# Turning the experts' products on VectorE, with a new cut of gate and up over TensorE's column groups

## What is computed

```python
combine = sum over the top 2 of one_hot(top_idx) * softmax(top_vals)
for e in range(8):                      # w_gu[e]: 1024 x 5632, w_down[e]: 2816 x 1024, f32
    gu = xt @ w_gu[e]
    g, u = gu[..., :2816], gu[..., 2816:]
    y = y + combine[:, e:e + 1] * ((silu(g) * u) @ w_down[e])
```

## Time and profile before

| | |
|---|---|
| median of three runs | 1141.8 us (1140.04 to 1142.01) |
| span of the profiled execution | 1140.8 us; no time beside the span is recorded for it |
| TensorE busy | 1100.7 us, 96% |
| VectorE, ScalarE busy | 309.3 us (27%), 233.6 us (20%) |
| first and last gate-up matmul of the experts | 444.6 and 1085.5 us |
| moved by DMA | 343.6 MB, mean 301 GB/s |

### The profile page before, as it was taken

How to read it: one execution, slowest core, us unless ns; L and a number is a source line. 1 busy time by engine, 2 the same in 40 slices (tenths; PEclk the granted TensorE clock), 3 DMA queues, 4 the chain that set the end, 5 groups by cost and what they waited for, 6 DMA issues and landing times.

```text
span 1140.8 us, 21118 instructions
## 1 busy us (share of the span) xinstructions
PE 1100.7 (96%) x9437; PEld 606.5 (53%) x9438; DVE 309.3 (27%) x536; ACT 233.6 (20%) x361; POOL 9.5 (1%) x53
## 2 busy tenths in 40 slices
PE   7889999999999899999999999999999999999988
PEld 5556999998688445344343353343343343433436
DVE  4664544444642515001100110100210101001053
ACT  3363444443522612000000000000000000000033
POOL 3000000000000000000000000000000000000000
PEclk9979999999999999999999999999999999999999
DMA  9806555555312309999999999999999999999951
GB/s 335 304 1 208 199 184 186 187 184 182 111 75 74 148 1 372 415 389 316 415 420 419 417 420 419 417 419 397 417 419 419 417 419 419 417 420 419 417 213 39
DMA packets 114024, 343.61 MB, mean 301 GB/s; under 512 B 7757, under 2 KB 30858, under 8 KB 113930
## 3 DMA queue, kind: packets, MB, share of 16 engines
q1 hardware_dynamic: 113930, 342.22, 76.6%
HBM read 341.15 MB, written 1.05 MB: 300 GB/s over the span
## 4 chain that ended last, share of the span: by engine, by line
PE 92%; DVE 4%; DMA 2%; ACT 1%; issue 0%; SPq 0%; DVEq 0%; ACTq 0%
PE ps L1958 34%; PE ps L2009 13%; PE ps L1666 6%; PE ps L1668 6%; PE ps L1667 6%; PE ps L2014 4%; PE ps L1636 4%; PE ps L1815 2%; DMA wring<-in_w_exp_down 1%; PE ps L1982 1%; PE ps L1937 1%; PE ps L2027 1%; PE ps L1527 1%; PE ps L1797 1%; PE ps L1740 1%; PE ps L1549 1%
## 5 line engine op out<-in xcount | busy, mean ns | idle before, releaser
L1958 PE MATMUL ps<-wring,xg 128*32 128x512 f32 (+1 forms) x4704 | 417.1, 502 | 1.5 <-DVE e_h L1368 1.5
L1958 PEld LDWEIGHTS ps<-wring,xg 128*32 128x32 f32 x4704 | 156.4, 110 | 241.6 <-issue 197.6
L2009 PE MATMUL ps<-wring,ehT 128*32 128x512 f32 x1408 | 167.0, 593 | 1.6 <-DMA wring<-in_w_exp_down 1.0
L1666 PE MATMUL ps<-dn_high,w_high 128*128 128x256 f32 x352 | 99.7, 283 | 0.0
L1668 PE MATMUL ps<-dn_high,w_low 128*128 128x256 f32 x352 | 99.6, 283 | 0.0
L1667 PE MATMUL ps<-dn_low,w_high 128*128 128x256 f32 x352 | 99.6, 283 | 0.0
L1124 DVE TENSOR_TENSOR w_low<-ring,w_high 128x2048 fp32r<-128x2048 f32 x36 | 82.3, 2291 | 60.0 <-ACT w_high L695 60.0
L2009 PEld LDWEIGHTS ps<-wring,ehT 128*32 128x32 f32 x1408 | 45.7, 110 | 97.1 <-issue 92.2
L829 ACT COPY ehT<-ps 128x384 f32<-128x384 f32 (+1 forms) x24 | 10.5, 439 | 364.9 <-PE ps L1982 276.0
L1380 DVE COPY ehT<-ps 128x384 f32<-128x384 f32 (+3 forms) x24 | 10.8, 450 | 262.6 <-PE ps L1982 201.7
L695 ACT CAST w_high<-ring 128x2048 fp32r<-128x2048 f32 x36 | 68.1, 1901 | 30.3 <-PE ps L1668 30.3
(11 more groups left out here) (311 smaller groups left out, 990.1 us busy)
## 6 DMA issues: line engine op xcount, KB each, us to landing
wring<-in_w_exp_gu SPq DMA_DIRECT2D x128, 1024.0 KB, 17.6
wring<-in_w_exp_down SPq DMA_DIRECT2D x88, 1024.0 KB, 16.3
wring<-in_w_exp_gu SPq DMA_DIRECT2D x64, 768.0 KB, 14.3
ring<-in_w_ffn_gu SPq DMA_DIRECT2D x44, 512.0 KB, 5.0
ring<-in_w_ffn_down SPq DMA_DIRECT2D x11, 1024.0 KB, 4.8
ring<-in_w_ple_gate SPq DMA_DIRECT2D x4, 1024.0 KB, 4.8
ring<-in_w_q_b SPq DMA_DIRECT2D x4, 1024.0 KB, 4.8
ring<-in_w_o_b SPq DMA_DIRECT2D x4, 1024.0 KB, 4.9
```

What stands on the lines that cost most here:

```text
L1666: pe.matmul(out, high_l, high_r, start=first, stop=False)
L1958: return pe.matmul(ps[32 * quarter:32 * quarter + 32, bank, c0:c0 + 2 * nf * P], xg[:, member(n), k, 32 * b:32 * b + 32], w[:, :, f * P:(f ...
L2009: ins = pe.matmul(ps[32 * q:32 * q + 32, 3, :], turned(g, 2 * u + r, b, nb), w[:, r, half * 512:(half + 1) * 512], start=(g == 0 and u == ...
```

## The change

TensorE's turns are gone, and with them banks 5 and 6, `e_h`, the copies to `ehT` and the semaphores `e_T`, `e_T_low` and `e_T_high`. VectorE multiplies in place in `e_silu` and then transposes 32x32 blocks from `e_silu` to `ehT`, which has two halves, for even and odd groups. A block on partitions 32j to 32j+31 stays on these partitions, so the hidden columns that column group j holds must be those that the down weights have on partitions 32j to 32j+31: it takes, of each block of 128, the run of 32 columns number j. In all three groups each column group now has one matmul a tile, of 2 x 32 x (number of blocks) columns: 512 and 384. Silu and product are one instruction for each group. Silu waits until the transpose has left `e_silu`; the transpose waits until the down units that read its half of `ehT` are done.

```diff
+    def products_of(buf, g, nb):
+        n = 32 * GROUPS[g][1]
+        return buf[:, 0:nb * n].rearrange("p (b n) -> p b n", b=nb)
...
         def silu(g, n, kind, nb):
             used(kind, "gu", g, n - 1 if kind == "body" and g < 2 else n)
-            if g < 2:
-                act.activation(e_silu[:, 0:2 * nb].rearrange("p (b c) n -> p b (c n)", b=nb), ps[:, 0:nb, 0:256], ACT.Silu).then_inc(e_silu_done, 1)
...
+            if not (isinstance(n, int) and n * 3 + g == 0):
+                act.wait_ge(e_turned, n * 3 + g)
+            act.activation(products_of(e_silu, g, nb), gates_of(g, nb), ACT.Silu).then_inc(e_silu_done, 1)
...
         def product(g, n, nb):
             dve.wait_ge(e_silu_done, n * 3 + (g + 1))
...
+            h_ = products_of(e_silu, g, nb)
+            dve.tensor_tensor(h_, h_, ups_of(g, nb), ALU.mult).then_inc(e_act_done, 1)
+
+        def turned(g, n, nb, kind):
+            dve.wait_ge(e_act_done, n * 3 + (g + 1))
+            if g == 2:
+                dve.wait_ge(e_used, n * EUNITS + used_count(kind, "down", 0))
+            elif not (isinstance(n, int) and n == 0):
+                dve.wait_ge(e_used, n * EUNITS + (used_count(kind, "down", 2 - g) - EUNITS))
+            m = nb * 32 * GROUPS[g][1]
+            dve.transpose(ehT[:, g % 2, 0:m], e_silu[:, 0:m]).then_inc(e_turned, 1)
...
         def both_experts(n):                 # VectorE
-            turned_high(1, n, nb)
             product(2, n, nb)
+            turned(2, n, nb, "body")
...
-            turned_high(2, n, nb)
             product(0, n + 1, nb2)
+            turned(0, n + 1, nb2, "body")
             result_low(n, nb)
             add_expert(n, n)
-            turned_high(0, n + 1, nb2)
...
             product(1, n + 1, nb2)
+            turned(1, n + 1, nb2, "body")
...
         def gate_up(kind, g, n, nb, ks=range(KD)):          # TensorE
-                if g < 2:
-                    for b in range(nb):
-                        for j in range(4):
-                            ins = part(j, b, 2 * j, 2, b, 0, first)
...
+                nf = GROUPS[g][1]
+                columns = w.rearrange("p s (f j a) -> p j s f a", j=4, a=32)
+                for b in range(nb):
+                    for j in range(4):
+                        ins = pe.matmul(ps[32 * j:32 * j + 32, b, 0:64 * nf], xg[:, member(n), k, 32 * b:32 * b + 32], columns[:, j],
+                                        start=first, stop=last, skip_group_check=True)
...
         def last_groups(n, nb, kind):                       # TensorE
             down(kind, 0, n, nb)
-            gate_up(kind, 2, n, nb, range(0, 4))
-            turn(1, n, nb)
-            gate_up(kind, 2, n, nb, range(4, KD))
+            gate_up(kind, 2, n, nb)
             down(kind, 1, n, nb)
-            turn(2, n, nb)
             down(kind, 2, n, nb)
             scatter(n, nb)
```

More of the change, by code:

```diff
@@ L1439, in _ @@
         product(0, 0, TILES[0])
-        turned_high(0, 0, TILES[0])
+        turned(0, 0, TILES[0], "lead")
         turn_picks(1)
@@ L1443, in _ @@
         product(1, 0, TILES[0])
+        turned(1, 0, TILES[0], "lead")
         for n in range(E - 1):
@@ L1955, in gate_up @@
                 first, last = k == 0, k == KD - 1
[L1957 to L1961, removed]
-                    for b in range(nb):
-                        for j in range(4):
-                            ins = part(j, b, 2 * j, 2, b, 0, first)
-                else:
-                    for b in range(nb):
-                        for j in range(4):
-                            part(j, b, j, 1, b, 0, first)
-                    for b in range(nb):
-                        for j in range(2):
-                            ins = part((2 * b + j) % 4, b, 4 + j, 1, b // 2, 256, False)
@@ L1972, in gate_up @@
-                ins.then_inc(e_used, 1)
-        def turn(g, n, nb):
-            pe.wait_ge(e_act_done, n * 3 + (g + 1))
-            if not (g == 0 and isinstance(n, int) and n == 0):
-                pe.wait_ge(e_T_low, n * 3 + g)
-                pe.wait_ge(e_T_high, n * 3 + g)
-                if g == 0:
-                    pe.wait_ge(e_added, n * 2)
-            for i in range(2 * nb if g < 2 else nb + 1):
-                ins = pe.transpose(ps[:, 5 + i // nb, (i % nb) * P:(i % nb + 1) * P], e_h[:, i, :], ident[:])
-            if g == 2 and nb == 3:
-                ins = pe.transpose(ps[:, 6, P:P + 64], e_h[0:64, 4, :], ident[0:64, 0:64])
-            ins.then_inc(e_T, 1)
@@ L2008, in down @@
                             q = 2 * half + b
-                            ins = pe.matmul(ps[32 * q:32 * q + 32, 3, :], turned(g, 2 * u + r, b, nb), w[:, r, half * 512:(half + 1) * 512],
+                            ins = pe.matmul(ps[32 * q:32 * q + 32, 3, :], turned(g, 2 * u + r, b), w[:, r, half * 512:(half + 1) * 512],
                                             start=(g == 0 and u == 0 and r == 0), stop=(end and r == 1))
@@ L2013, in down @@
                         q = 2 * half + r
-                        ins = pe.matmul(ps[32 * q:32 * q + 32, 4, :], turned(g, 2 * u + r, 2, nb), w[:, r, half * 512:(half + 1) * 512],
+                        ins = pe.matmul(ps[32 * q:32 * q + 32, 4, :], turned(g, 2 * u + r, 2), w[:, r, half * 512:(half + 1) * 512],
                                         start=(g == 0 and u == 0), stop=end)
```

84 lines of the change are left out of this document (23 added, 61 removed).

## The result

| | before | after |
|---|---|---|
| median, five runs each on one chip | 1142.01 us (1140.04 to 1145.96) | 1136.39 us (1135.72 to 1138.22) |
| span of the profiled execution | 1140.8 us | 1135.4 us |
| first gate-up matmul of the experts | 444.68 | 443.27 |
| first down unit of group 1, last expert ("T" below) | 1086.85 | 1080.80 |
| from the one to the other | 642.17 | 637.53 |

The changed kernel takes 0.9953 of the time of the one before (95% interval 0.9935 to 0.997): faster by 0.5%. The forecast was 1138.0.

A forecast was written before the change was run, and what follows sets the result against it. The prediction took the weights' transfers, not TensorE, to set the time from 550 us on. Terms of -3.7, -1.6 and +1.7 us summed to -3.6, 1137.2 us for the profiled span, carried to a median of 1138.0; range 1133 to 1145.

The forecast's parts named there:

- rival C: Expert stage: the stream isn't at its limit and runs ahead when TensorE frees buffers 29 us sooner: 1113 us, chance 0.03.
- the hole: Fall of the transfer rate at 515 to 540 us, to 238 GB/s at worst, with 6.8 us lacking in all.
- (a): TensorE's turns, one in each of the 24 groups: their removal saves 20.2 us of TensorE's work.
- (b): Third group's gate and up matmuls: 1.93 us a unit with three tiles, 1.29 with two; 8.9 us of TensorE's work saved.
- (c): Groups 0 and 1: reading the moving operand in runs of 32 columns costs TensorE nothing; taken as zero.
- Rival A: Gate and up matmuls: runs of 32 columns slow TensorE's reads; 1152 us if by 10%, chance 0.12.
- VectorE: 24 added transposes of up to 768 columns, taken at 0.95 us each, are hidden and add nothing to the sum.
- Term 1: Transfers at 515 to 540 us: TensorE's earlier releases move the stream behind by 3.7 us, bounds 0 and 6.8.
- Term 2: Tail, between the fourth and fifth of the last seven down units: the last turn goes, saving 1.6 us.
- Term 3: TensorE's longer wait before the last down weights brings a low clock, costing 1.7 us, bounds 0 and 3.4.
- B: No change: the pause before the last down weights costs more clock, or the stream moves less than 3.7 us: 1140.5, chance 0.17.
- D: The dip at 515 to 540 us closes wholly and no clock is lost: -8.4 us, 1133.4, chance 0.08.

The follow-up runs named there:

- experiment 5: The changed kernel with each of the 24 transposes of the eight experts issued twice, one after the other: ratio 0.9953 to the kernel before.
- turns_first: The changed kernel with TensorE's turns of the first expert's groups 0 and 1 put back twice each as unread dummies: ratio 0.9991 to the kernel before.
- turns_back: The changed kernel with unread dummy turns put back on TensorE at all 24 old places, once each: 1141.85 us, ratio 0.9988 to the kernel before.
- after_again: The changed kernel itself, unedited, run once more beside later kernels: 1138.56 us, ratio 0.9968 to the kernel before.
- gates_2_2: The changed kernel with two of the last gate's four 1 MB loads moved behind the last down weights, engine steps split to match: ratio 0.9946 to before.
- gates_2_2b: Differs from gates_2_2 only in the order of VectorE's and ScalarE's steps: 1133.88 us, ratio 0.9917 to the kernel before.

## Why the prediction was right, point by point

**The bound.** Right. With TensorE idle for 10.9 of 500 us the stream still runs at 419 GB/s, so rival C (1113 us) is out; and 15 us of TensorE put back behind the hole move T by 0.5.

**(a) The turns and (b) group 2.** Right: 672 fewer gate-up matmuls, no turn, 1.935 us a unit against 1.93, 1.29 against 1.29. The fullest column group sets a unit's cost, as the prediction counted it.

**(c) The runs of 32 columns.** Right: 20.60 us for eight units of 512 columns in three tiles is 2.575 a unit, and 593 ns an instruction, both as before. Rival A (1152 us) is out. The Trainium skill, Advanced Engine Details and Errata, Memory Cachelines, has full rate for accesses that stay within a 16-byte line of SBUF, and this trace agrees; the slowdown which it puts down to non-contiguous patterns under PSUM doesn't show for the moving operand from SBUF (593 ns).

**VectorE.** Right: 978 ns for 0.95 us, and off the path (experiment 5).

**Term 1, 3.7 us.** Right in its size by the end of the first hole, 3.8 (3.4 in the repeat, with 411 and 364 GB/s); and the claim under it, that the releases ahead of the hole move the whole stream one to one, is shown by `turns_first` (3.8 in, 3.9 out). Two parts were off. Of the 3.8, 1.3 lay in the 70 us ahead of the hole, where the prediction allowed 0.2. And T moved by 4.6: some 0.8 of it is a second place, at 770 to 785 us, where the backlog ran out before. The step that failed is "there is always a backlog", which I read from one median over 500 us; that median was 17.1 and the local one 10.8. The cost of the step is this 0.8 to 1.1 us. With all turns back and the new group 2 (`turns_back`) this place still runs at 419 GB/s, so it needed the old cut of group 2; whether that alone would do stays open, since it wasn't tried.

**Term 2, 1.6 us.** Right: the seven units stand without a gap.

**Term 3, +1.7 us.** The mechanism was right and its size too small: 3.64 + 1.42 against 1.92 + 0.86 is 2.3 us. I took the 3.4 us low stretch of the earlier trace rows; here it was 6.8 us long, of which 2.2 fell into the wait (1078.6 to 1080.8) and 4.6 into work. TensorE: Matmul & The Clock Gate of the Trainium skill, HAM oscillation, has a loop that waits 3 to 5 us for DMA at each step and starts slowly behind each wait. The long wait of 6.8 us agrees (0.50 behind it); the 20 short ones, at most 1.5 us, are shorter than the page's, and the clock stayed at 1.00.

**The waits.** I had 17 us of short waits and 8 to 10 of a long one; measured were 10.9 and 6.8. Of the 27.5 us freed, 4.6 are T's, 10.9 the short waits and 5.8 the growth of the long one, from 1.0. Of the 6.2 left, TensorE's restart after a stop is some 4.6 by estimate: 0.20 us each (the earlier trace rows has 0.20 for the first unit behind the turn) for 23 more stops from 926 us to T than the kernel before has. The other 1.6 us stay open. The long wait is shorter than 8 us because of TensorE's own lag: the weights of T land five 1 MB transfers, some 12.5 us, behind group 2's last, and TensorE ended that one only 5.7 us after it had landed (12.5 - 6.8, worked out).

**The sum.** From T's shift, the turn and the clock: -4.6 - 1.6 + 2.3 = -3.9 us in the trace, forecast -3.6. That the two are so near is in part luck: T moved by 0.9 more than forecast and the clock cost 0.6 more, and the two errors have opposite signs. The medians differ by 5.6 in the first comparison and by 3.9 in the second (`after_again`, 1138.56 against 1142.42). The forecast was 3.8 under the median before, so the second comparison meets it, and in the first the time came out 1.6 us under 1138.0. Rivals B (1140.5) and D (1133.4) lie on either side of both; D's closed hole and lost-nothing clock did not come (4.5 us of the hole stayed, and the clock fell).

## What to carry to other kernels

Where a stream of weights sets the time, an edit on the engine that consumes them is worth only what it does at the places where the stream runs dry: find these by the rate in short stretches, not by a median over the whole stage and not by the issuing queue's waits alone, which took 38.9 of 70 us in `turns_back` with nothing lost there. 3.8 us at one place took the gain away, and 15 us elsewhere hardly touched it. Once the consumer has slack, look at what else stands in the queue ahead of the last needed transfer (here 4 MB for a later stage), and when moving it, order the other engines' strict queues by when each input lands: the same two loads moved gave a ratio of 0.9946 in one order of VectorE's and ScalarE's steps and 0.9917 in the other, where the changed kernel had 0.9953 and 0.9968. Count landmarks from an event inside the trace, because the start of a stage can move by more than the effect.

## What the runs showed of the hardware that I had not expected

- TensorE's clock took 20 stops of up to 1.5 us within 100 us in the changed kernel, and one of 2.2 us in `gates_2_2` and of 2.4 in `gates_2_2b`, without leaving 1.00; behind the stops of 5.9 to 7.1 us it was at 0.50 for 6.8 to 6.9 us. The length of a stop alone doesn't tell: in the kernel before, one stop of 2.14 us, around 333 us, was followed by the low level.
- Filling the long stop with matmuls kept the clock up there. A low level of 0.70 over 5 us came 22 us later, over the scatter, in the one trace that there is.
- SP waited for TensorE's releases during 38.9 of 70 us in `turns_back` while the stream ran at 419 GB/s; during 47.3 of 70 in the kernel before it fell to 372 GB/s over 5 us.
- A moving operand in 16 runs of 32 f32 reads at the same 593 ns as one in two runs of 256.
- A 32x32 block transpose of 128x768 f32 takes VectorE 978 ns, hardly more than the 955 ns of a product of that size; 578 ns for 384 columns.
